# The differences and sums of the seven-product feed-forward: from GpSimd to VectorE

## The reference

```python
def swiglu(x, w_gu, w_down):           # x: 512 x 1024
    g, u = jnp.split(x @ w_gu, 2, axis=-1)   # w_gu: 1024 x 5632, so g and u are 512 x 2816
    return (jax.nn.silu(g) * u) @ w_down     # w_down: 2816 x 1024
```

## Time and profile before

| | |
|---|---|
| median of the runs | 3047.17 us |
| the profiled execution | 3049.26 us |
| its span | 3047.5 us |
| TensorE matmul busy | 2891.3 us (95%) |
| VectorE busy | 1655.5 us (54%) |
| ScalarE busy | 1265.2 us (42%) |
| GpSimd busy | 585.4 us (19%) |
| mean granted TensorE clock | 0.98 |

### The profile page before, as it was taken

One profiled execution on the slowest core, in us unless ns is written; L12 is line 12 of the kernel. 1 busy time (PEld: TensorE's weight loads), 2 busy tenths in 40 slices (PEclk: granted clock), 3 DMA queues, 4 the chain that ended last, 5 costly groups with the idle time before them and its releaser, 6 DMA issues.

```text
span 3047.5 us, 43223 instructions
## 1 busy us (share of the span) xinstructions
PE 2891.3 (95%) x18236; PEld 2534.4 (83%) x18236; DVE 1655.5 (54%) x2087; ACT 1265.2 (42%) x2081; POOL 585.4 (19%) x325
## 2 busy tenths in 40 slices
PE   7999999999999979999998999997999999989998
PEld 6888887788888779888777998887998876889987
DVE  4364343333335786644668656247655458676653
ACT  3323234444444344432654444234444248444441
POOL 1000000020000054500004442024440011054410
PEclk9999999999999999999999999998999999989999
DMA  5323222222222213233221323351323330222331
GB/s 197 131 98 110 97 97 83 84 77 77 76 86 72 97 63 104 84 111 101 69 70 56 99 96 111 104 148 56 104 91 111 85 96 2 70 69 93 101 108 72
DMA packets 186258, 278.68 MB, mean 91 GB/s; under 512 B 29578, under 2 KB 127034, under 8 KB 185936
## 3 DMA queue, kind: packets, MB, share of 16 engines
q1 hardware_dynamic: 177024, 247.17, 25.1%
q0 software_dynamic: 9040, 28.73, 3.0%
HBM read 271.56 MB, written 4.25 MB: 91 GB/s over the span
## 4 chain that ended last, share of the span: by engine, by line
PE 64%; DVE 13%; DMA 7%; issue 6%; POOL 6%; ACT 3%; POOLq 0%; SPq 0%; DVEq 0%; ACTq 0%
PE bank L664 17%; PE bank L666 17%; PE bank L665 17%; DMA raw<-in_ffn_w_gu 6%; POOL raw L2555 3%; POOL xt_spare L2555 3%; DVE w_low L2249 2%; DVE w_high L2249 2%; PE bank L802 2%; PE bank L890 1%; PE bank L858 1%; DVE sum L2260 1%; PE bank L874 1%; PE bank L822 1%; PE bank L811 1%
## 5 line engine op out<-in xcount | busy, mean ns | idle before, releaser
L1894 DVE TENSOR_TENSOR w_low<-raw,w_high 128x2048 fp32r<-128x2048 f32 (+1 forms) x132 | 296.1, 2243 | 663.5 <-ACT w_high L1450 657.1
L1450 ACT ACTIVATE w_high<-raw 128x2048 fp32r<-128x2048 f32 (+1 forms) x132 | 247.2, 1874 | 529.4 <-PE bank L666 522.9
L664 PE MATMUL bank<-xt_high,w_high 128*128 128x512 f32 (+1 forms) x1128 | 407.8, 361 | 3.7 <-DVE w_high L2249 2.8
L666 PE MATMUL bank<-xt_high,w_low 128*128 128x512 f32 (+1 forms) x1128 | 402.6, 357 | 0.0
L665 PE MATMUL bank<-xt_low,w_high 128*128 128x512 f32 (+1 forms) x1128 | 399.2, 354 | 0.0
L2523 POOL TENSOR_TENSOR small<-small 128x1 f32<-128x1 f32 (+1 forms) x43 | 25.3, 588 | 1233.4 <-DVE small L1919 1195.0
L664 PE MATMUL bank<-w_high,hidden_high 128*128 128x512 f32 x640 | 249.3, 390 | 0.0
L666 PE MATMUL bank<-w_high,hidden_low 128*128 128x512 f32 x640 | 249.0, 389 | 0.0
L665 PE MATMUL bank<-w_low,hidden_high 128*128 128x512 f32 x640 | 249.0, 389 | 0.0
L664 PEld LDWEIGHTS bank<-xt_high,w_high 128*128 128x128 f32 x1128 | 213.3, 189 | 40.7 <-issue 12.5
L666 PEld LDWEIGHTS bank<-xt_high,w_low 128*128 128x128 f32 x1128 | 216.6, 192 | 31.2
(11 more groups left out here) (439 smaller groups left out, 7681.2 us busy)
## 6 DMA issues: line engine op xcount, KB each, us to landing
raw<-in_ffn_w_gu SPq DMA_DIRECT2D x80, 1024.0 KB, 5.3
raw<-in_ffn_w_down SPq DMA_DIRECT2D x44, 1024.0 KB, 4.9
raw<-in_b_w_in SPq DMA_DIRECT2D x40, 1024.0 KB, 5.1
raw<-in_a_w_in SPq DMA_DIRECT2D x24, 1024.0 KB, 5.1
raw<-in_a_w_out SPq DMA_DIRECT2D x8, 1024.0 KB, 4.9
raw<-in_ffn_w_gu SPq DMA_DIRECT2D x16, 512.0 KB, 5.5
raw<-in_w_out SPq DMA_DIRECT2D x5, 1024.0 KB, 5.0
raw<-in_w_mem_kv SPq DMA_DIRECT2D x4, 1024.0 KB, 5.3
```

Of the source, the lines that this page charges most:

```text
L664: pe.matmul(o, lh, rh, start=start, stop=False, skip_group_check=True)
L666: return pe.matmul(o, ll, rh, start=False, stop=stop, skip_group_check=True)
L1450: act.activation(homes[n][0][:, 0:w], RAW[n % 2][:, 0:w], ACT.Copy).then_inc(sem["w_high_ready"], step("w_high_ready", n))
L1894: dve.tensor_tensor(homes[n][1][:, 0:w], RAW[n % 2][:, 0:w], homes[n][0][:, 0:w].bitcast(F32), ALU.subtract).then_inc(sem["w_low_ready"], ...
```

## The change

The four differences of each unit move to VectorE, each at the step of the loop before the low part that needs it: 3 and 2 of the next unit at the end of product 4's step, 4 of the next unit at product 6's step, 6 of this unit after the low part of factor 5 at product 0's step. Difference 2 gets a tile of its own. Sum 3 moves to VectorE too; GpSimd only adds the high and the low parts of the two quarters of the first 256 tokens (`join_quarters`, two additions), as soon as these tokens are ready. Sum 2 is then sum 1 less sum 3's joined quarter, and sums 1 and 2 are made ahead of low parts 0 and 1, sums 3 and 4 after them, between the low parts of the first unit. ScalarE's order follows.

```diff
-            low(0)
-            low(1)
-            token_sums()
-            for n in SUM_ORDER:
-                dve.wait_ge(sem["sum_high"], at("sum_high", (f, n)))
-                ... (sum_low of all four sums)
+            token_sum(1)          # three additions
+            token_sum(2)          # one, waits for quarter_joined 3
+            low(0)
+            low(1)
+            difference(1, 3)
+            difference(1, 2)
+            sum_low(2)
             ... (unit 0: hidden, two halves)
-            low(3)
-            low(2)
-            low(4)
+            low(2)
+            sum_low(1)
+            low(3)
+            token_sum(3)          # two
+            difference(1, 4)
             for q in range(count):
                 ... (what follows product q)
+                if q == 0:
+                    sum_low(3)
+                    low(4)
+                    token_sum(4)  # two, waits for quarter_joined 4
+                if q == 1:
+                    sum_low(4)
+                if n == 4 and u + 1 < UNITS:
+                    difference(u + 1, 3)
+                    difference(u + 1, 2)
+                if n == 6 and u + 1 < UNITS:
+                    difference(u + 1, 4)
                 if q + 5 < count:
                     low(q + 5)
+                if n == 0:
+                    if u == 1:
+                        dve.wait_ge(sem["product_done"], ...)
+                    difference(u, 6)
```

```diff
-            for n in SUM_ORDER:      # ScalarE: all four sums ahead of unit 0's activations
-                ... sum_high(n)
+            sum_high(2)
             for j in range(2):
                 ... (unit 0: silu of banks 0 and 1)
+            high(2)
+            sum_high(1)
             high(3)
-            high(2)
-            high(4)
             for q in range(count):
                 ... (what follows product q)
+                if q == 0:
+                    sum_high(3)
+                    high(4)
+                if q == 1:
+                    sum_high(4)
                 if q + 5 < count:
                     high(q + 5)
```

```diff
-        def differences(l, i, s):    # GpSimd: sum 3, then four differences per unit
+        def join_quarters(l, i, s):
             f = (l, i)
+            pool.wait_ge(sem["xt_ready"], at("xt_ready", (s, 1)))
+            for n, k0 in ((3, 0), (4, 4)):
+                pool.tensor_tensor(FFN[f]["sum"][n][:], XTH[:, k0:k0 + 4, 0:256].bitcast(F32), XTL[:, k0:k0 + 4, 0:256].bitcast(F32),
+                                   ALU.add).then_inc(sem["quarter_joined"], ...)
```

More of the change, by code:

```diff
@@ L105 @@
     x_loaded3 xt_ready y_high_ready y_multiplied y_split p_scaled
-    unit_done factor_high factor_ready sum_ready sum3_ready sum_high sum_split snapped gate_summed unit_gated unit_hidden differences
+    unit_done factor_high factor_ready sum_ready quarter_joined sum_high sum_split snapped gate_summed unit_gated unit_hidden differences
     slopes_ready pair_done pair_high pair_split  cmp_v_spread cmp_halves_done cmp_halves_read fold_ready gates_turned gates_taken gates_t_read
@@ L257, in unit_tiles @@
         tiles["slot"] = at("unit_slot", [P, 2048], slot, F32R)
+        tiles["difference"] = at("difference", [P, 4, 256], spare)
         tiles["hidden"] = [at(f"hidden{u}", [P, 2, SEQ], b) for u, b in enumerate(hidden)]
@@ L428, in factor @@
         slot = FFN[f]["slots"][q % 5]
-        src = (gate_raw[:, 0:1024], gate_raw[:, 1024:2048], DIFF2, gate_raw[:, 0:1024], up_raw[:, 0:1024],
+        src = (gate_raw[:, 0:1024], gate_raw[:, 1024:2048], FFN[f]["difference"][:], gate_raw[:, 0:1024], up_raw[:, 0:1024],
                up_raw[:, 1024:2048], DIFF4)[n]
@@ L437, in unit_banks @@
         return (ps[4], ps[0], ps[1]) if u % 2 else (ps[7], ps[6], ps[5])
-    DIFF2, DIFF4 = (SPARE[i][:, 0:4, 256:512] for i in range(2))
+    DIFF4 = SPARE[0][:, 0:4, 256:512]
     slopes = alibi_slopes(HEADS)
@@ L1724, in ffn, with sum_high @@
             high(1)
-            for n in SUM_ORDER:
[L1726 to L1729, removed]
+            def sum_high(n):
+                act.wait_ge(sem["sum_ready"], at("sum_ready", (f, n)))
                 act.activation(tiles["sum_high"][n][:], tiles["sum"][n][:],
                                ACT.Copy).then_inc(sem["sum_high"], step("sum_high", (f, n)))
+            sum_high(2)
             for j in range(2):
@@ L2250, in low, with x @@
                                   ALU.subtract).then_inc(sem["factor_ready"], step("factor_ready", key))
[L2252 to L2271, removed]
+            def x(high, k0, t0):
+                return (XTH if high else XTL)[:, k0:k0 + 4, t0:t0 + 256].bitcast(F32)
@@ new lines, in token_sum @@
+            def token_sum(n):
+                out = tiles["sum"][n][:]
+                if n == 1:
+                    link(dve.tensor_tensor(out, x(True, 0, 256), x(True, 4, 256), ALU.add))
+                    link(dve.tensor_tensor(out, out, x(False, 0, 256), ALU.add))
+                    ins = dve.tensor_tensor(out, out, x(False, 4, 256), ALU.add)
+                if n == 2:
+                    dve.wait_ge(sem["quarter_joined"], at("quarter_joined", (f, 3)))
+                    ins = dve.tensor_tensor(out, tiles["sum"][1][:], tiles["sum"][3][:], ALU.subtract)
+                if n == 3:
+                    link(dve.tensor_tensor(out, out, x(True, 0, 256), ALU.subtract))
+                    ins = dve.tensor_tensor(out, out, x(False, 0, 256), ALU.subtract)
+                if n == 4:
+                    high, low2 = tiles["sum_high"][2][:].bitcast(F32), tiles["sum_low"][2][:].bitcast(F32)
+                    dve.wait_ge(sem["quarter_joined"], at("quarter_joined", (f, 4)))
+                    link(dve.tensor_tensor(out, out, high, ALU.subtract))
+                    ins = dve.tensor_tensor(out, out, low2, ALU.subtract)
+                ins.then_inc(sem["sum_ready"], step("sum_ready", (f, n)))
+                dve.wait_ge(sem["sum_ready"], at("sum_ready", (f, n)))
@@ new lines, in sum_low, with difference @@
+            def sum_low(n):
+                dve.wait_ge(sem["sum_high"], at("sum_high", (f, n)))
+                dve.tensor_tensor(tiles["sum_low"][n][:], tiles["sum"][n][:], tiles["sum_high"][n][:].bitcast(F32),
+                                  ALU.subtract).then_inc(sem["sum_split"], step("sum_split", (f, n)))
+            def difference(u, n):
+                g, up = ids["unit", l, i, u]
+                b11, b21 = RAW[g % 2][:, 0:1024], RAW[g % 2][:, 1024:2048]
+                b12, b22 = RAW[up % 2][:, 0:1024], RAW[up % 2][:, 1024:2048]
+                t2 = tiles["difference"][:].rearrange("p k n -> p (k n)")
+                deep = lambda b: b.rearrange("p (k n) -> p k n", k=4)
+                if n == 3:
+                    dve.wait_ge(sem[f"panel_loaded{up % 2}"], at(f"panel_loaded{up % 2}", up))
+                    dve.wait_ge(sem["factor_ready"], at("factor_ready", (f, u, 0)))
+                    ins = dve.tensor_tensor(b11, b12, b11, ALU.subtract)
+                if n == 2:
+                    if u > 1:
+                        dve.wait_ge(sem["factor_ready"], at("factor_ready", (f, u - 1, 2)))
+                    ins = dve.tensor_tensor(t2, b22, b11, ALU.subtract)
+                if n == 4:
+                    ins = dve.tensor_tensor(b12, b22, b12, ALU.subtract)
+                if n == 6:
+                    if u > 1:
+                        dve.wait_ge(sem["factor_ready"], at("factor_ready", (f, u - 1, 6)))
+                    ins = dve.tensor_tensor(DIFF4, deep(b21), tiles["difference"][:], ALU.subtract)
+                ins.then_inc(sem["differences"], step("differences", (f, u, n)))
+                dve.wait_ge(sem["differences"], at("differences", (f, u, n)))
@@ L2278, in ffn @@
             prepare(ids["first", l, i][-1])
+            dve.wait_ge(sem["xt_ready"], at("xt_ready", (s, TT - 1)))
+            token_sum(1)
+            token_sum(2)
             low(0)
             low(1)
-            token_sums()
-            for n in SUM_ORDER:
-                dve.wait_ge(sem["sum_high"], at("sum_high", (f, n)))
-                dve.tensor_tensor(tiles["sum_low"][n][:], tiles["sum"][n][:], tiles["sum_high"][n][:].bitcast(F32),
-                                  ALU.subtract).then_inc(sem["sum_split"], step("sum_split", (f, n)))
+            difference(1, 3)
+            difference(1, 2)
+            sum_low(2)
             for j in range(2):
@@ L2319, in ffn @@
                                       ALU.mult).then_inc(sem["unit_hidden"], step("unit_hidden", (f, u, 1)))
+                if q == 0:
[9 more added lines that the diff above has]
+                    difference(u + 1, 4)
                 if q + 5 < count:
                     low(q + 5)
+                if n == 0:
+                    if u == 1:
+                        dve.wait_ge(sem["product_done"], at("product_done", ("panel", ids["first", l, i][1])))
+                    difference(u, 6)
                 if u == UNITS - 1:
```

(14 more changed lines are left out.)

## The result

The changed kernel takes 3070.07 us (median; 3069.33 to 3071.90), the kernel before 3046.77 us in the runs beside it (3044.32 to 3047.51). The ratio is 1.0079, 95% interval 1.0061 to 1.0096: slower by about 23 us. The forecast was 3069.5.

What follows compares the result with a forecast made beforehand. A loop outside TensorE, from panel load through ScalarE, GpSimd and VectorE, was taken to set the pace at 22.47 us per unit. 48.5 - 27.0 + 0.8 = +22.3 us gave 3069.5 us, range 3055 to 3088.

Steps and rivals of the forecast that it cites:

- The loop of before: Old kernel's units: a loop outside TensorE, from up panel issue to the next, 22.4 us by rows, 22.47 measured.
- The term: Units' new loop through the gate load: 23.99 us, 1.52 more than 22.47, over 32 units +48.5 us.
- The differences at 1.22 on VectorE, L2312 at 0.68: VectorE in the units: moved differences take 1.22 us each, and L2312 falls from 2.18 to 0.68 without GpSimd beside it.
- Two loads out together: SyncE's queue in the units: gate and up panel loads issued 0.4 us apart, before 2.87 us apart.
- TensorE stops twice per unit, ahead of 2 and 5: TensorE in the units: idle ahead of products 2 and 5, about 1.8 us each.
- The start: Start of the four feed-forwards, up to product 2 of unit 2: 5.7 to 7.1 us won each, together -27.0 us.
- The additions on GpSimd: GpSimd's two additions beside the last row block: row done 2.2 us later but hidden, 0, bounds 0 and +6 us.
- The end: End of each feed-forward: the down panel's load waits for difference 6 too, holding snapshot 4; +0.8 us in all.
- The sum: Whole kernel: 48.5 - 27.0 + 0.8 = +22.3 us on the profiled 3049.3, 3071.6; less 2.1 for the median, 3069.5.
- The rival that ended on the other side: Units: differences find VectorE idle, the loop falls below 20.2 us, TensorE's seven products set the pace; 2948 us, chance 0.13.
- The two rivals on the loads' landing times: Panel loads: slow landings come only from staggered issues, no change (3048, 0.10); or paired loads share the rate (3184, 0.07).
- two levels: Panel loads' landing times: 5.1 to 5.4 and 6.1 to 6.6 us from an issue; basis of the no-change rival, 0.10.

Runs made afterwards that it cites:

- the fourth kernel: ScalarE's snapshot of product 3 put ahead of high part 0 of the next unit, against the changed kernel: 3061.60 us, ratio 1.0052 to the kernel before.

## Why the prediction was right

- *The loop of before* (22.4 by rows) was read rightly; the same list of durations in the new order gave 23.99, measured 23.87. The term came out at +44.6 in place of +48.5. What is off is the start of difference 3 after the gate's issue: 9.33 forecast, 9.05 on the mean of the 32 turns. High 0 began 5.08 to 6.42 us after the issue, mean 5.33 (5.50 forecast). I had put the up panel later than the gate's chain in 9 of 32 turns; VectorE stood idle for it in 3, all in the third feed-forward (0.35 to 0.60 us). The other part of the loop is 14.82 (14.66).
- *The differences at 1.22 on VectorE, L2312 at 0.68*: 1.22 and 0.69. Two loads out together, 0.41 us apart: right.
- *TensorE stops twice per unit, ahead of 2 and 5*: right in 22 of the 32 units, 2.0 and 1.4 us in the common turn (1.8 each forecast), and in 10 the second stop went into TensorE's slower work; that they cost nothing by themselves is shown by the fourth kernel.
- *The start*: -27.0 forecast, -27.1 measured; the idle time ahead of product 4 is 5.4 us (5.2), but 8.8 us in the third feed-forward, which I had not worked out. The same wait ends it there: difference 6 (2096.36 to 2097.58), high 6 (2097.61), snapshot 2 (2098.58), product 4 (2099.23). TensorE was only ready for it sooner, 14.4 us after low 0 began in place of 18.2.
- *The additions on GpSimd*: hidden, as said. Their touch on VectorE's operation was 0.8 us in the first feed-forward and 2.1 in the second and fourth, within the 2.2 that I had allowed.
- *The end*: +0.8 forecast; +2.0 with all else behind the starts and outside the units, and +0.6 ahead of the first feed-forward, neither taken apart.
- *The sum*: that 3069.5 is within 1 us of 3070.07 is luck. Between the two profiled executions I had +22.3 and their spans show +20.1: the loop came 3.9 short, what I had at 0.8 or left out came to 2.6. The median of the changed kernel then lay 0.5 us above its profiled execution, where I had taken the 2.1 below of the kernel before.
- *The rival that ended on the other side* (TensorE becomes the bound, 2948) had the mechanism and its price right, but not in this kernel: it holds as soon as difference 6 is moved ahead of the two low parts before it (2956). The point that I named for it, the place of difference 6 ahead of the gate load, decides. The two rivals on the loads' landing times found nothing for them. One of them rested on "two levels" of the landing times, and that reading was wrong, as the last section says.

## What to carry to other kernels

Moving work to a faster engine with idle time says nothing until the work is placed in that engine's list: follow the loop from one load's issue to the next, and put what releases the load into a stretch in which the engine waits anyway. Take the stops of the busiest engine as symptoms until a loop through it is shown: here one move that removed such a stop gained 8 us while a load set the pace and cost 29 us when the engine did. When a loop is shortened, look for the next one with the same list in hand before combining two good edits.

## What the runs showed of the hardware

Of the 288 gate panel loads (1 MB) of units 3 to 10 in the nine traces, 239 land less than 5.5 us after their issue (from 4.92 on), 19 after 5.5 to 6 and 30 after 6 to 6.98. The prediction had two levels; there is one common time with a tail. Before, I could not say whether the late ones came from the second load 2.87 us behind. With the loads 0.41 us apart they are there too (6.40), and with 2.5 us between them (6.86), so the distance to the next load is not their cause; what is remains open. The up panel's landing, counted from the gate's issue, has a median of 8.16 us with 0.41 us between the two issues, 9.02 with 1.21, 8.18 with 2.48 and 8.79 with 2.87 (32 turns each); this order is unexplained.

Of the shared port: an addition on VectorE beside one on GpSimd took 1.98 us here, 3.42 in the earlier trace rows, depending on how much of GpSimd's was left when it began, as a lock would have it (the Trainium skill, SBUF — State Buffer, two separate sides). The trace agrees: GpSimd's first addition ended at 1055.17, and VectorE's, begun at 1054.27, ended at 1056.25, 1.08 us after that, close to its 1.22 alone.
